# Two later layers of a three-layer block: values by token, scaled rotary tables, and half a convolution on ACT and POOL

## The chip, the cores and the metric

One core of one Trainium2 chip. The metric is the device time of one launch in microseconds. The median of three runs of the kernel before is 2020.88 us (2020.03 to 2021.06). Engines: PE is TensorE, DVE VectorE, ACT ScalarE, POOL GpSimd, SP SyncE.

## The reference, cut to what matters

A first block (a pooling mixer, a sparse attention of three branches, a gated feed-forward layer) works on 512 tokens of width 1024; two later layers follow. The change touches only the first part of each later layer: the input projection and the mixing that hangs on it.

```python
def mixing_layer(h, cos, sin, w_in, ...):
    u = jnp.einsum("bsd,de->bse", h, w_in)                # h = rmsnorm(x, mix_norm_g)
    a_b, a_c, a_x, q, k, v, c_in = jnp.split(u, offs, axis=-1)
    y_a = a_b * causal_depthwise_conv(a_c * a_x, short_conv_w)          # 3 taps, 256 wide
    q = apply_rope(q.reshape(b, s, 2, 4, 64), cos, sin)
    k = apply_rope(k.reshape(b, s, 2, 4, 64), cos, sin)
    o = diff_attention(q, k, v.reshape(b, s, 4, 128), lam)  # softmax(m=0) - lam * softmax(m=1)
    y_b = rmsnorm(o, diff_subln_g) * (1.0 - lam_init)
    c = c_in + glu_b
    c = c[..., :256] * jax.nn.sigmoid(c[..., 256:])
    c = causal_depthwise_conv(c, conf_dw_w) + conf_dw_b     # 31 taps, 256 wide
    y_c = jax.nn.silu(layernorm(c, conf_ln_g, conf_ln_b))
    return jnp.einsum("bse,ed->bsd", jnp.concatenate([y_a, y_b, y_c], -1), w_out)
```

## The kernel before

**Layout and arithmetic.** Everything is held feature by feature: 128 features on the partitions, the 512 tokens along a row. A weight chunk is eight blocks of 128x128 floats; it is split into a high part (`wh`, made by ACT with one copy, `head`) and the rest (`wl`, made by POOL in `rest` as two halves of 512 columns, `raw - wh`, L421). The input is split as well (`xh`, `xl`). A tile of 128 output features is three products over eight blocks: `wh` with `xh` (L450), `wh` with `xl` (L451), `wl` with `xh` (L470), 24 matmuls of 512 columns, into one PSUM bank. PE needs POOL's part only for the last eight. `wh` and `wl` hold two chunks each: ACT may write chunk n+2 when chunk n is done, and POOL subtracts chunk n+2 after that. Four semaphores carry this: `raw_landed`, `hi_ready`, `lo_ready`, `chunk_done`.

**Order of a later layer.** The order on each engine is written out by hand; there is no planner. The input projection takes 22 chunks. The first four are a group (`group`, L507, L508, L514): they fill four banks together, so that the feature blocks of the input are consumed as they come, and give `ca` and `cg`, the two halves of the gated unit (`glu`, L1731). Chunks 4 to 15 give, for each of four heads, a q tile, a k tile and a v tile; chunks 16 to 21 give the short convolution's tiles `a_c`, `a_x`, `a_b`, twice. Tiles go alternately to banks `G[0]` and `G[1]`; PE may start tile n when DVE has read tile n-2 (`tile_out`). After it come the output projection (eight chunks, the first four as a group in the order of rows `Y_ORDER`), the feed-forward layer's 44 chunks and its down projection.

**What is done beside the projection.** PE opens two slots in each chunk, one after the first eight matmuls and one after the first four low ones (`slot`, `layer_slots`). A head has steps 0 to 10, one in each half-chunk: steps 0 to 3 compute scores of one block of 128 queries (L839, L841), DVE takes the maxima (`peak`, L1739), ACT the exps (L1176), DVE combines the two softmaxes one step later (`combine`, L1746, L1748, L1252), PE transposes the result two steps later (L851), ACT copies it (`put`). Step 6 multiplies with the values (L858), steps 7 to 10 norm the head and split it into `yh`, `yl`. A score's step also waits until the exps of the step before have read its banks. Heads start every six half-chunks, at slot 14.

**Rotation.** DVE takes a q or k tile out of its bank times the norm's scale `rstd` into `ybuf` (`take`, L1295; with 0.125 for q, L1255) and multiplies it with `cos2` into `tmp3` (L1811). PE rotates `ybuf` with a matrix (`rotate_l`, L828), and DVE multiplies with `sin2` and adds (`rot_end`, L1708, L1710). A v tile is taken in the same way, transposed by PE (`turn_v`, L816) and copied by ACT into `lv`.

**The 31-tap convolution** runs on DVE alone for both groups of 128 channels (`taps`, L1722 and L1252, 2 x 31 instructions of 128x512 a layer), between the steps by a written plan (`TAP_PLAN`). Before dependent operations DVE has an explicit drain (L1718 and others).

## Time and profile before

| | |
|---|---|
| median of three runs | 2020.88 us |
| the profiled execution's own time | 2020.96 us |
| its span, first to last instruction | 2019.2 us |
| mean granted TensorE clock | 0.981 |
| busy: PE, DVE, ACT, POOL | 1930.6 (96%), 990.2 (49%), 690.8 (34%), 880.9 us (44%) |
| layer 1: first matmul of the group, end of chunk 3, first matmul of the output projection | 764.08, 787.2, 970.92 us |
| layer 2: the same stage | 1381.56 to 1591.06 us |

How to read it. A row of a window gives its length, then for each engine busy time and, in brackets, the number of instructions, then the granted clock (1.00 is full), the share of the DMA engines and GB/s. A row of waits says who waited, for whom, the total in us, how often, and the longest. A row of instructions by line gives the tile written and the tiles read, the shape, the count, then busy us and the mean ns of one, and the idle time of the engine just before them with what ended it. A row of a source view gives minimum, median and maximum ns. A row of the timeline gives start and length in us, and in square brackets the idle time before it. PEld is the weight load, POOLq the sequencer of POOL. A line such as L1252 is a helper's (`fma`) and serves several callers; the tile tells them apart.

### The profile page before, as it was taken

What the parts mean: (1) busy time and instruction counts of PE and PEld (TensorE: products, weight loads), DVE (VectorE), ACT (ScalarE), POOL (GpSimd) and SP (SyncE); (2) the same over time, 40 slices, a digit from 0 to 9 for tenths busy, and PEclk for the clock granted to TensorE, in tenths of its full rate; (3) what the DMA queues carried; (4) which work ended last, traced back from release to release, by engine and by line L of the source; (5) the groups of instructions that cost most, each with busy time, mean ns of one, the idle gap of its engine ahead of it and who ended that gap; (6) DMA issues with size and microseconds to landing.
All of it is one profiled execution on the core that took longest, in us unless ns stands there. A gap on an engine that the chain in (4) does not pass through costs nothing.

```text
span 2019.2 us, 28668 instructions
## 1 busy us (share of the span) xinstructions
PE 1930.6 (96%) x8702; PEld 1521.7 (75%) x8702; DVE 990.2 (49%) x1398; ACT 690.8 (34%) x1084; POOL 880.9 (44%) x630
## 2 busy tenths in 40 slices
PE   6999999999999998988999999999897999999996
PEld 5866678878888887656888888887565888888885
DVE  7667654466664214886443333123878343333213
ACT  4245553333232222344433333223243343232222
POOL 4222224446555554322445455454222344554554
PEclk9999999999999999999999999999899999999998
DMA  6111112222222332111222322332111222222232
GB/s 238 63 53 43 43 63 94 94 84 93 95 103 94 104 104 84 53 47 52 80 94 93 102 95 93 104 104 95 52 45 51 73 90 98 93 93 97 101 104 83
DMA packets 48952, 173.89 MB, mean 86 GB/s; under 512 B 5488, under 2 KB 6512, under 8 KB 48624
## 3 DMA queue, kind: packets, MB, share of 16 engines
q1 hardware_dynamic: 48880, 172.96, 25.6%
q8 instruction: 42, 0.69, 0.1%
q14 instruction: 30, 0.25, 0.0%
HBM read 169.82 MB, written 2.10 MB: 85 GB/s over the span
## 4 chain that ended last, share of the span: by engine, by line
PE 85%; DVE 7%; DVEq 4%; issue 2%; ACT 2%; DMA 0%; ACTq 0%; SPq 0%
PE bank L450 21%; PE bank L470 21%; PE bank L451 21%; PE bank L507 3%; PE bank L514 3%; PE bank L508 3%; DVEq L1718 1%; PE bank L484 1%; PE bank L684 1%; PE bank L490 1%; PE bank L485 1%; DVEq L1810 1%; PE bank L713 1%; PE bank L531 1%; PE bank L727 1%
## 5 line engine op out<-in xcount | busy, mean ns | idle before, releaser
L421 POOL TENSOR_TENSOR wl<-raw,wh x626 | 880.7, 1428 | 1124.6 <-ACT wh L919 1124.4
L919 ACT ACTIVATE wh<-raw 128x1024 fp32r (+1 forms) x313 | 331.8, 1060 | 872.0 <-PE bank L470 740.5
L450 PE MATMUL bank<-xh,wh 128*128 128x512 f32 x1400 | 565.6, 404 | 5.6 <-DVE tmp L1295 5.6
L451 PE MATMUL bank<-xl,wh 128*128 128x512 f32 x1400 | 554.1, 396 | 0.0
L470 PE MATMUL bank<-xh,wl 128*128 128x512 f32 x1400 | 359.9, 396 | 0.0
L450 PEld LDWEIGHTS bank<-xh,wh 128*128 128x128 f32 x1400 | 268.7, 192 | 67.5 <-issue 7.0
L451 PEld LDWEIGHTS bank<-xl,wh 128*128 128x128 f32 x1400 | 268.9, 192 | 60.6 <-issue 4.9
L470 PEld LDWEIGHTS bank<-xh,wl 128*128 128x128 f32 x1400 | 262.6, 190 | 56.3 <-issue 3.0
L450 PE MATMUL bank<-hh,wh 128*128 128x512 f32 x528 | 208.0, 394 | 0.0
L451 PE MATMUL bank<-hl,wh 128*128 128x512 f32 x528 | 208.0, 394 | 0.0
L1295 DVE TENSOR_TENSOR ybuf<-bank,rstd 128x512 f32<-128x512 f32 x111 | 76.2, 687 | 231.3 <-PE bank L470 229.3
L1664 DVE TENSOR_TENSOR tmp<-tmp,ybuf 128x512 f32<-128x512 f32 x66 | 109.8, 1664 | 74.3 <-ACT tmp L1136 74.1
L1626 DVE TENSOR_TENSOR xs<-xs,bank 128x512 f32<-128x512 f32 (+1 forms) x48 | 32.1, 684 | 226.4 <-PE bank L470 178.0
L470 PE MATMUL bank<-hh,wl 128*128 128x512 f32 x528 | 134.8, 394 | 0.0
L451 PEld LDWEIGHTS bank<-hl,wh 128*128 128x128 f32 x528 | 98.7, 187 | 24.5
L450 PEld LDWEIGHTS bank<-hh,wh 128*128 128x128 f32 x528 | 98.7, 187 | 24.4
L470 PEld LDWEIGHTS bank<-hh,wl 128*128 128x128 f32 x528 | 98.7, 187 | 24.4
L1252 DVE SCALAR_TENSOR_TENSOR conv<-cpad,par,conv 128x512 f32<-128x512 f32 x120 | 102.0, 891 | 6.7 <-issue 2.1
L507 PE MATMUL bank<-xh,wh 128*128 128x512 f32 x192 | 76.7, 400 | 9.4 <-ACT wh L919 8.5
L919 ACT ACTIVATE hh<-tmp 128x512 f32 (+1 forms) x66 | 41.7, 632 | 120.3 <-DVE tmp L1664 120.3
L1666 DVE TENSOR_TENSOR hl<-tmp,hh 128x512 f32 (+1 forms) x66 | 51.1, 774 | 59.8 <-ACT hh L919 59.8
L508 PE MATMUL bank<-xl,wh 128*128 128x512 f32 x192 | 75.8, 395 | 0.0
(273 smaller groups left out, 2099.4 us busy)
## 6 DMA issues: line engine op xcount, KB each, us to landing
raw<-in_weights SPq DMA_DIRECT2D x313, 512.0 KB, 3.3
xs<-in_x SPq DMA_DIRECT2D x4, 512.0 KB, 6.9
out_t<-xs SPq DMA_DIRECT2D x8, 256.0 KB, 2.2
w1k<-in_w SPq DMA_DIRECT2D x1, 1024.0 KB, 9.5
w1v<-in_w SPq DMA_DIRECT2D x1, 1024.0 KB, 10.5
shifted<-kvraw SPq DMA_DIRECT2D x8, 124.0 KB, 2.4
posi<-in_positions SPq DMA_DIRECT2D x2, 256.0 KB, 8.6
cst<-in_consts SPq DMA_DIRECT2D x1, 290.0 KB, 5.2
```

What stands on the lines that cost most here:

```text
L421: x_ = pool.tensor_tensor(wl[:, :, :].rearrange("p s n -> p (s n)")[:, two], raw[:, cols((v % 4) * (CB * P) + h * half, half)], wh[:, :, : ...
L450: mm(b[:, :], w, kh(k), start=first and k == 0, stop=False)
L451: mm(b[:, :], w, kl(k), start=False, stop=False)
L470: i = mm(b[:, :], wl[:, s, (blk0 + k) * P:(blk0 + k + 1) * P], kh(k), start=False, stop=last and k == blocks - 1)
L507: mm(X4[a][:, :], w, kh(k), start=k == 0, stop=False)
L508: mm(X4[a][:, :], w, kl(k), start=False, stop=False)
L514: i = mm(X4[a][:, :], wl[:, s, (4 * kk + a) * P:(4 * kk + a + 1) * P], kh(2 * c + kk), start=False, stop=c == 3 and kk == 1)
L919: return act.activation(o, i, ACT.Copy, scale=scale)
L1252: return stt(out=o, in0=a, scalar=s, in1=b, op0=ALU.mult, op1=ALU.add)
L1295: return tt(o, b[:, :], rstd[:, :], ALU.mult).then_inc(tile_out, 1)
L1664: tt(tmp[:, 1, :], tmp[:, 0, :], ybuf[:, 0, :], ALU.mult).then_inc(R["prod_ready"], 1)
L1666: tt(flat(hl)[:, cols(j * S, S)], tmp[:, 1, :], flat(hh)[:, cols(j * S, S)].bitcast(F32), ALU.subtract).then_inc(R["h_lo"], 1)
```

## The change

Only the later layers change.

1. **Values token by token.** Chunks 4 to 7 are one group, `vgroup`: the input's token block is the stationary operand and 512 weight columns move, so four banks receive tokens on the partitions and all four heads' values along a row. ACT copies them into `lv`, each token with its own scale (`s_recip`). `turn_v` and DVE's takes of v are gone. The weights are laid out anew for it.
2. **Rotary tables hold the norm's scale.** DVE multiplies `cos2` and `sin2` once a layer with the broadcast scale into `cosr`, `sinr`. ACT copies a raw q or k tile from its bank to `ybuf`; DVE multiplies the bank with `cosr` into `tmp3`, and that frees the bank.
3. **Half the convolution off VectorE.** Channels 0 to 127 stay on DVE (one instruction a tap, with most taps before the first rotary tile). For channels 128 to 255 ACT makes each tap's product into `tprod` (two buffers) and POOL adds it, between its subtractions, from chunk 5 on: three taps a chunk up to chunk 9, then two.
4. **A head every four half-chunks**, starting at slot 21 of 43 (two slots a chunk, counted from the first chunk). Older heads go first in a slot, and PE's transposes stand ahead of the scores. The values' products go to bank `ROT` in place of `OUT`. The norm's statistics are numbered anew, and `Y_ORDER` is changed so that head 3 is the fifth row.

```diff
-HEAD0 = 7
-Y_ORDER = ("head0", "head1", "head2", "ya0", "head3", "ya1", "conv0", "conv1")
+HEAD_SLOT = 21
+Y_ORDER = ("head0", "head1", "ya0", "head2", "head3", "ya1", "conv0", "conv1")
@@ layer_slots
-        s = 2 * (n - HEAD0) + half
-        yield s, [(h, s - 6 * h) for h in (3, 2, 1, 0) if 0 <= s - 6 * h <= 10]
+        s = 2 * n + half
+        yield s, [(h, s - HEAD_SLOT - 4 * h) for h in range(4) if 0 <= s - HEAD_SLOT - 4 * h <= 10]
@@ gpsimd
+                def tap(k):
+                    if k == 0:
+                        pool.tensor_scalar(conv[:, 1, :], cpad[:, 1, 0:S], c2("dw_w", TAPS), c2("dw_b", 1),
+                                           ALU.mult, ALU.add)
+                    else:
+                        pool.drain()
+                        pool.wait_ge(R["tap_prod"], Count(k).loop(l, TAPS - 1).value())
+                        pool.tensor_tensor(conv[:, 1, :], conv[:, 1, :], tprod[:, k % 2, :], ALU.add)\
+                            .then_inc(R["tap_added"], 1)
+                done = 0
+                for n in range(T_LIN):
+                    if n == 5:
+                        pool.wait_ge(R["glu_out"], Count(1).loop(l, 1).value())
+                    rest(T + n)
+                    if n >= 5:
+                        upto = min(done + (3 if n < 10 else 2), TAPS)
+                        for k in range(done, upto):
+                            tap(k)
+                        done = upto
@@ tensor
+            def vgroup(t, n, hooks):
+                for c in range(4):
+                    s = (t + c).even()
+                    pe.wait_ge(hi_ready, (t + (c + 1)).value())
+                    for i in range(NT):
+                        if c == 0 and i >= 2:
+                            pe.wait_ge(tile_out, (n + (i - 1)).value())
+                        for kk in range(2):
+                            k = 2 * c + kk
+                            w = wh[:, s, kk * S:(kk + 1) * S]
+                            mm(VB[i][:, :], xh[:, k, i * P:(i + 1) * P], w, start=k == 0, stop=False)
+                            mm(VB[i][:, :], xl[:, k, i * P:(i + 1) * P], w, start=False, stop=False)
+                    pe.wait_ge(lo_ready, (t + (c + 1)).value())
+                    for i in range(NT):
+                        for kk in range(2):
+                            k = 2 * c + kk
+                            x_ = mm(VB[i][:, :], xh[:, k, i * P:(i + 1) * P], wl[:, s, kk * S:(kk + 1) * S],
+                                    start=False, stop=k == KD - 1)
+                    x_.then_inc(chunk_done, 1)
...
@@ scalar
+                def products(n):
+                    for k in range(made[0], min(made[0] + n, TAPS)):
+                        if k == 1:
+                            act.wait_ge(R["glu_out"], L1.value())
+                        if k > 2:
+                            act.wait_ge(R["tap_added"], Count(k - 2).loop(l, TAPS - 1).value())
+                        copy(tprod[:, k % 2, :], cpad[:, 1, k:k + S], scale=c2("dw_w", TAPS + k))\
+                            .then_inc(R["tap_prod"], 1)
+                    made[0] += n
...
+                        if n >= 5:
+                            products(2 if n < 10 and half == 0 else 1)
...
+                    if 8 <= n < 16:
+                        i, m = n - 8, n - 4
+                        if i >= 2:
+                            act.wait_ge(rot_ready, Count(6 + i).loop(l, 8).value())
+                        b = QK0[i] if i < 2 else G[(N + m).even()]
+                        copy(ybuf[:, i % 2, :], b[:, :]).then_inc(R["rope_in"], 1)
                     head(T + (n + 2))
+                    if n == 7:
+                        act.wait_ge(recip_ready, (U0 + 1).value())
+                        for i in range(NT):
+                            copy(lv[:, :, i, :], VB[i][:, :].rearrange("p (h d) -> p h d", d=P),
+                                 scale=s_recip[:, i:i + 1]).then_inc(R["v_out"], 1)
@@ vector
-                TAP_PLAN = {4: (2, 1), 5: (1, 1), 6: (2, 1), 19: (2, 2)}
+                TAP_PLAN = {4: (0, 2), 5: (2, 2), 6: (2, 2), 7: (2, 2), 8: (2, 2), 9: (2, 2)}
...
+                tt(cosr, BC[:, :], cos2[:, :], ALU.mult)
+                tt(sinr, BC[:, :], sin2[:, :], ALU.mult).then_inc(bc_read, 1)
...
-                        take(tl, nl_, ybuf[:, n % 2, :], scale=0.125 if what == 0 else None)
-                        if what < 2:
-                            dve.drain()
-                            tt(tmp3[:, 0:S], ybuf[:, n % 2, :], cos2[:, :], ALU.mult)
+                        dve.wait_ge(R["rope_in"], Count(i + 1).loop(l, 8).value())
+                        if i % 2:
+                            tt(tmp3[:, 0:S], b[:, :], cosr, ALU.mult).then_inc(tile_out, 1)
+                        else:
+                            mul3(tmp3[:, 0:S], b[:, :], 0.125, cosr).then_inc(tile_out, 1)
```

## Rows read from the trace of the kernel before

**Rows 1.** The page, part 4: shares of the chain that ended last.

```profile
PE 85%; DVE 7%; DVEq 4%; issue 2%; ACT 2%; DMA 0%; ACTq 0%; SPq 0%
```

**Rows 2.** Windows: layer 1's stage, its part after chunk 10, layer 2's stage.

```profile
764.08:970.92 206.84, 182.42 (x832) 135.12 (x830) 146.60 (x229) 73.95 (x142) 63.92 (x45) 0.95 0.17 59
854.95:970.92 115.97, 101.34 (x476) 73.89 (x474) 84.73 (x134) 45.40 (x90) 31.43 (x22) 0.96 0.15 51
1381.56:1591.06 209.50, 185.08 (x831) 137.16 (x832) 146.47 (x229) 73.62 (x142) 63.40 (x44) 0.93 0.18 59
```

**Rows 3.** Windows: one bare chunk, and one head period of three chunks.

```profile
787.20:792.66 5.46, 5.46 (x25) 4.50 (x24) 4.04 (x6) 3.68 (x4) 2.54 (x2) 1.00 0.26 98
844.27:876.13 31.86, 28.23 (x135) 19.64 (x135) 26.39 (x44) 13.93 (x30) 9.23 (x6) 1.00 0.17 57
```

**Rows 4.** Waits of PE over the whole span.

```profile
PE bank L828 <- DVE ybuf L1295: 14.8, 6, 2.8
PE bank L828 <- DVE ybuf L1255: 10.5, 2, 5.2
PE bank L851 <- DVE lp L1252: 9.7, 2, 4.9
...
PE bank L839 <- ACT lp L1176: 6.4, 8, 1.0
PE bank L816 <- DVE ybuf L1295: 6.0, 4, 2.0
```

**Rows 5.** PE by line in the same period: the value transposes.

```profile
L816 PE MATMUL bank<-cst,ybuf 128*128 128x128 f32 x4 | 0.6, 272 | 0.0
```

**Rows 6.** DVE by line in the head period of rows 3.

```profile
L1252 DVE SCALAR_TENSOR_TENSOR conv<-cpad,par,conv 128x512 f32<-128x512 f32 x12 | 9.5, 832 | 0.7 <-issue 0.2
L1739 DVE TENSOR_REDUCE small<-bank 128x1 f32<-128x128 f32 (+3 forms) x8 | 3.5, 481 | 1.5 <-PE bank L841 1.5
L1748 DVE TENSOR_SCALAR lp<-lp,small 128x128 f32<-128x128 f32 (+3 forms) x4 | 3.3, 814 | 0.3
L1811 DVE TENSOR_TENSOR tmp<-ybuf,cos 128x512 f32<-128x512 f32 x2 | 2.6, 1315 | 0.2
L1252 DVE SCALAR_TENSOR_TENSOR lp<-lp,small 128x128 f32<-128x128 f32 (+3 forms) x4 | 2.2, 552 | 0.3
L1708 DVE TENSOR_TENSOR tmp<-bank,sin 128x512 f32<-128x512 f32 x2 | 1.4, 684 | 0.0
L1295 DVE TENSOR_TENSOR ybuf<-bank,rstd 128x512 f32<-128x512 f32 x2 | 1.4, 680 | 0.0
...
L1272 DVE RECIPROCAL small<-small 128x4 f32<-128x4 f32 x1 | 0.2, 178 | 2.3 <-ACT small L936 2.3
```

**Rows 7.** ACT by line in layer 1's stage: a 128x512 copy.

```profile
L919 ACT ACTIVATE yh<-lo__109 128x512 fp32r<-128x512 f32 x4 | 2.5, 627 | 0.9 <-DVEq L1769 0.9
```

**Rows 8.** Source views of L421 and L1252, whole span: ns min/median/max.

```profile
L421 POOLq FUSED_REGOPS  x939: 57/74/161, 8.5 to 2002.7; - x188
...
L421 POOL TENSOR_TENSOR wl<-raw,wh x626: 1262/1292/1933, 8.9 to 2004.0; - x157
...
L1252 DVE SCALAR_TENSOR_TENSOR conv<-cpad,par,conv x120: 739/750/1853, 794.4 to 1561.6; 128x512 f32<-128x512 f32 x120
```

**Rows 9.** Timeline of DVE and POOL in layer 1, 791 to 798 us.

```profile
791.11 2.12 DVE L1731 SCALAR_TENSOR_TENSOR cpad<-ca,par,cg 128x512 f32<-128x512 f32 x2 [1.20 <-ACT cg L1210]
...
794.57 1.69 POOL L421 TENSOR_TENSOR wl<-raw,wh  x1 [2.56 <-ACT wh L919]
...
795.06 1.75 DVE L1252 SCALAR_TENSOR_TENSOR conv<-cpad,par,conv 128x512 f32<-128x512 f32 x1
...
796.89 1.59 DVE L1252 SCALAR_TENSOR_TENSOR conv<-cpad,par,conv 128x512 f32<-128x512 f32 x1
```

**Rows 10.** Timeline of PE in layer 1: a late stall, and a layer norm's sums.

```profile
941.14 0.44 PE L851 MATMUL bank<-cst,lp 128*128 128x128 f32 x1 [4.87 <-DVE lp L1252]
...
954.96 1.84 PE L531 MATMUL bank<-cst,conv 128*128 128x1 f32 x16
```

More of the change, by code:

```diff
@@ L425, in rest @@
                 x_.then_inc(lo_ready, 1)
-            with pool.Fori(0, T_ALL + 2) as t:
+            with pool.Fori(0, T_BLOCK1) as t:
                 rest(Count(0).loop(t, 1))
+            with pool.Fori(0, LAYERS) as l:
+                T = Count(T_BLOCK1).loop(l, T_LAYER)
+                def tap(k):
[17 more added lines that the diff above has]
+                        done = upto
+                with pool.Fori(T_LIN, T_LAYER) as t:
+                    rest(T.loop(t, 1))
+            for t in range(T_ALL, T_ALL + 2):
+                rest(Count(t))
         @block.tensor
@@ L803, in lam_sum @@
                     pe.wait_ge(R["lam_in"], L1.value())
[L804 removed]
+                    pe.wait_ge(tile_out, (N + 3).value())
+                    mm(TR[:, 0:2], ones, lamp, start=True, stop=True).then_inc(R["lam_psum"], 1)
                 RO = Count(7).loop(l, 8)
@@ L893, in slot @@
-                    if s == 26:
-                        pe.wait_ge(R["conv_done"], L1.value())
-                        ln_stats(U0 + 5, conv)
-                    if s == 27:
-                        spread(U0 + 5, lambda i: s_recip[:, i:i + 1].to_broadcast([P, P]))
-                    if s == 28:
+                    if half == 0 and 9 <= n < 17:
+                        rotate_l(n - 9)
+                    if s == 38:
+                        pe.wait_ge(R["conv_done"], L1.value())
+                        pe.wait_ge(R["tap_added"], Count(TAPS - 1).loop(l, TAPS - 1).value())
+                        ln_stats(U0 + NORM_LN[0], conv)
@@ L904, in _ @@
                 xgroup(T, feed, {(1, 1): lambda: x_stats(U0, feed), (2, 0): lambda: x_spread(U0)})
-                for n in range(4, T_LIN):
-                    xk(T + n, N + n, slots=[lambda: slot(n, 0), lambda: slot(n, 1)], lag=5 if n < 6 else 1)
-                tb, nb = out_and_ffn(T + T_LIN, N + T_LIN, (yh, yl), (R["y_lo"], Count(0).loop(l, KD)), U0 + 7,
+                vgroup(T + 4, N, {(1, 0): lam_sum})
+                for m in range(4, N_LIN):
+                    n = m + 4
+                    if m == 4:
+                        pe.wait_ge(R["lam_exp"], L1.value())
+                    if m == 6:
+                        pe.wait_ge(R["v_out"], Count(NT).loop(l, NT).value())
+                    xk(T + n, N + m, slots=[lambda: slot(n, 0), lambda: slot(n, 1)],
+                       lag={4: 0, 5: 1, 6: 2, 7: 3}.get(m, 1), bank_=QK0[m - 4] if m < 6 else None)
@@ L1212, in _ @@
                 for n in range(4, T_LIN):
-                    for s, steps in layer_slots(n):
-                        if n == 6 and s % 2 == 0:
+                    for half, (s, steps) in enumerate(layer_slots(n)):
+                        if s == 11:
                             act.wait_ge(R["lam_psum"], L1.value())
-                            act.activation(lame, POOLB[:, 0:2], ACT.Exp).then_inc(R["lam_exp"], 1)
+                            act.activation(lame, TR[:, 0:2], ACT.Exp).then_inc(R["lam_exp"], 1)
+                        if s == 38:
+                            act.wait_ge(R["ya_ready"], Count(1).loop(l, 2).value())
+                            y_head("ya0", ya[:, 0, :])
@@ L1699, in _ @@
                 ts(sub_gain, c2("sub_g"), c2("lam_init", 1), None, ALU.mult)
-                x_norm(U0)
+                recips(U0, NT)
+                dve.wait_ge(bc_ready, (U0 + 1).value())
+                dve.tensor_copy(rstd[:, :], BC[:, :])
+                dve.memset(sqacc[:, :], 0.0)
+                dve.drain()
                 SS = Count(4 * NU).loop(l, 32)
```

169 lines of the change are left out of this document (85 added, 84 removed).

## The prediction

> **What bounds the kernel now.** First the page: the chain that ended last is 85% TensorE (PE) [rows 1], so time is lost where PE waits. The change touches only the input projection of the two later layers, so next come the windows of those stages: layer 1 from the first matmul of its group to the first of the output projection, 206.84 us, and layer 2, 209.5 us [rows 2]. In them PE is busy 182.4 and 185.1 us, at a mean granted clock of 0.95 and 0.93 of full. A bare chunk of 24 matmuls takes 5.46 us [rows 3]; 22 of them are 120 us, the rest is attention and losses. The waits of PE name the cause: the rotation L828 waits for `ybuf` from VectorE (DVE) 14.8 + 10.5 us, the transposes L851 of the probabilities 9.7, the scores L839 for exps 6.4, the value transposes L816 6.0 [rows 4]. These lines exist only in these two stages: 47.4 of the 48.8 us that PE is idle there. DVE is not full, but works in order: in one head period of three chunks (844.27 to 876.13) it is busy 26.39 of 31.86 us, PE 28.23, ScalarE (ACT) 13.93, GpSimd (POOL) 9.23 [rows 3].
>
> **The change, part by part.**
>
> *Values token by token.* The four value tiles become one group with the same 96 matmuls of 512 columns: no change for PE. What goes is `turn_v`, 0.6 us a head [rows 5], and its wait, 3.0 us a layer. DVE loses four takes of 0.68 [rows 6]. ACT still makes four copies of a bank, now scaled. Two of the group's banks are free, two come free with the first two takes, 0.7 and 1.4 us after its start, and are needed after 1.8 and 2.7. Hidden under the first two banks' matmuls; were DVE late, the price is one take.
>
> *Rotary tables with the scale in them, raw copy on ACT.* Two DVE products more a layer, 1.4 us after the GLU, when nothing waits for DVE. Per rotated tile DVE does one product from the bank in place of a take and a product; ACT adds a copy, eight a layer, 0.63 each by its nearest row [rows 7]. The rotation no longer waits for DVE but for ACT, which stands behind two exps and a tap product there. Of the 12.6 us a layer of L828 some 9 go; I leave 0.8 a head.
>
> *Channel 1 of the convolution on ACT and POOL.* DVE loses 31 taps of 0.75 [rows 8]. ACT gains 30 products of 0.63. POOL gains 31 operations of 128x512, the shape of its own halves: 1.29, from 1.26 to 1.93 [rows 8]. Before nearly each stand a drain, register work and a wait, which the halves don't have: at least the 0.07 of one FUSED_REGOPS, at most what the slowest half takes over the usual, 0.64; I take 0.3, half way. A tap is 1.3 to 2.6 then, and I take 1.6 alone.
>
> The rows show that this is free for neither engine. While POOL subtracts, DVE's taps take 1.75 and 1.59 in place of 0.75, and POOL's half 1.69 in place of 1.29 [rows 8, 9]: side by side, one of each goes through in about 1.7. The Trainium skill (SBUF — State Buffer, "SBUF: two separate sides") calls the pair of ports that both use an exclusive lock for a whole instruction, where the loser "fully blocks". By that a pair would cost 0.75 + 1.29 = 2.04; the trace's 1.7 is softer, in the same direction.
>
> DVE's channel 0 is pulled ahead: 18 taps stand before the first rotary tile with nothing to hold them, so from 794 DVE runs them back to back at 1.75, until 825.5. POOL's part of chunks 5 to 9 is two halves and three taps: beside DVE's taps 3.4 + 3 x 2.0 = 9.3 us (rounded down), afterwards 2.6 + 3 x 1.6 = 7.4. PE's bare chunk is 5.46, so POOL bounds chunks 6 to 10. On layer 1's clock: the GLU ended at 793.2 beside POOL [rows 9], and ends at 792.7 without; only then may POOL subtract chunk 5, done 795.9, needed 796.3: hidden. Its taps last until 801.1. Low parts are ready for chunk 6 at 804.5, 7 at 813.8, 8 at 823.1; then, DVE being done, 5.4 + 2.9 and 4.8 + 2.9 (one meeting each left): 9 at 831.3, 10 at 839.0. The eight low matmuls (a third of 5.46) and one score (0.6, an estimate from the four transposes of [rows 5]) later chunk 10 ends, 841.4. Before it ended at 854.95: a gain of 13.5. PE alone would be there at about 828.
>
> *A head every four half-chunks, from slot 21.* Eleven chunks remain. PE's work: the old period has 28.23 busy for three chunks and one head; less `turn_v` 0.6 and a chunk 5.5 that is 22.1 for two chunks and a head, so 11.1 of attention a head. Sum: 11 x 5.5 = 60.5; four heads 44.4, less the slot of it already done, 2.8; the layer norm's two sums of 1.84 [rows 10] and two spreads of 0.5, 4.7: 106.8.
>
> DVE in the new period: 26.39, less all conv taps 9.5, less three takes 2.0 and two cos products 2.6, plus two taps 1.5 and two products 1.4: 15.2 [rows 3, 6]. In the old period POOL's six operations cost DVE, on L1811, 2.6 for 1.4, and on the conv taps, 9.5 for 9.0; on L1748 about 1.2 of its 3.3: 2.9 in all, 0.5 each. POOL now has eight in a shorter period: 4 in place of L1748's 1.2 makes 18. ACT: 13.93 plus four products and two copies of 0.63, at most 17.7. PE binds with 22.1, but three in-order engines hand over in every slot. What is late next: the first score of a head stands one slot (5.5 us of PE) behind its own key's rotation. In that slot DVE first waits 2.3 for the root of the head two before, then has its reciprocal 0.2, a combine 1.4, a peak 1.0, a tap 0.8, the rotation's end 1.4 [rows 6], and one meeting with POOL 0.5: 7.6, so 2.1 late for two of four heads, 1.05 a period. With 0.8 for the rotation and 0.5 for exps that is 2.4 a period: 24.5, and over 3.5 periods 8.4. The stall behind the short convolution's block (4.87 at 941.14 [rows 10]) moves; I leave 3 for it. After chunk 10: 106.8 + 8.4 + 3 = 118.2; before 115.97 [rows 2]. This part gives back 2.2: the old losses were small here.
>
> *Order of heads and rows.* Head 3 ends in the last half-chunk; the output projection takes it as its fifth row, 10.9 us on, `conv0` at 16.4. Hidden under its first two chunks; without them one DVE subtraction, 0.7. SP's queue keeps number and size of its loads. POOL's program is longer, for which no row has a price: 0, bounded by 3 us (a start of a chunk missed in each layer).
>
> **Sum.** Layer 1: 841.4 + 118.2 = 959.6 against 970.92, gain 11.3. Layer 2 has the same program: twice, 22.6. The profiled execution takes 2020.96 for its span of 2019.2, and the median is 2020.88, so nothing is carried over. 2020.9 - 22.6 = 1998.3; I say 1999.
>
> Unknowns: POOL's tap at 1.3 in place of 1.6 is 4 us a layer (-8), at 2.6 its ends come up to 12 later (+24). A period without losses is -8.4 a layer (-17); its ceiling is a rival.
>
> **Rivals.**
>
> *PE-bound (0.26).* Waits spread DVE and POOL so that they meet little, and the hand-overs hide. For it: PE's 22.1 over DVE's 18. Against it: DVE's unheld taps. POOL alone still needs 7.4 a loop, so chunk 10 ends at 835; then 106.8: 941.8, gain 29.1 a layer: 1963.
>
> *DVE bound under POOL (0.17), the other side.* In a period DVE has 13 operations that read SBUF for both inputs, or one input at double rate (combine 8, rotation's ends 2, taps 2, a remainder 1). If all meet POOL at 0.95 each, as 0.75 became 1.7 [rows 9]: 15.2 - 1.2 + 12.4 = 26.4, and with the idle 2.3 for the root 28.7. Four heads cost 4.2 more each, 16.8 a layer: 976.4, 5.5 later than before: 2032. It decides from a period of 27.3 on. Against it: POOL idles about half of a period.
>
> *The lock as that page has it (0.09).* Each of DVE's 18 taps costs POOL 0.35 more, 6.3 a layer, and about 5 again in the attention part: 11.3 a layer, 2021, no change. It is the skill's sentence that asks for it (same page and section); the rows of 1.7 speak against.
>
> **How the numbers follow.** Forecast (about 1985 to 2014) 0.48. Within 0.2% (4 us) a measurement can't tell from no change. Faster: 0.48 + 0.26 = 0.74. Same: 0.07, of the lock. Slower: 0.17 + 0.02 = 0.19. The range takes in the PE-bound case and stops short of 2032: 1961 to 2026.
>
> **What would show it.** In chunks 6 to 10 of each later layer PE waits for `wl` before the low matmuls, 2 to 4 us each, POOL is at 90%, DVE's taps take 1.6 to 1.75, and chunk 10 ends 54 us after chunk 3. L816 is gone. Where the rotation waits, it is for ACT. Head periods are 24 to 25 us, the first score of heads 2 and 3 waits for `lk`. The stages take 196 and 198 us. It is wrong if chunks 6 to 10 take 5.5 us each (POOL's tap is cheaper or hidden), or if a period is above 27 with DVE full.

## The result, and the profile after

The changed kernel takes 1987.1 us (median of 4 runs, 1985.0 to 1989.4) against 2021.0: the ratio is 0.9828, 95% interval 0.9814 to 0.9843, and the medians are 33.9 us apart. The prediction said 1999 (1961 to 2026). The profiled execution takes 1989.08 for its span of 1987.3.

The page of the changed kernel, its first and fourth parts (beside [rows 1]): VectorE (DVE) is busy 25.8 us less, ScalarE (ACT) 44.5 and GpSimd (POOL) 89.5 us more; in the chain, the share of DVE's sequencer is halved and POOL's sequencer is new.

```profile
PE 1918.2 (97%) x8670; PEld 1515.1 (76%) x8670; DVE 964.4 (49%) x1316; ACT 735.3 (37%) x1160; POOL 970.4 (49%) x692
...
PE 81%; DVE 6%; POOLq 3%; issue 3%; DVEq 2%; ACT 2%; POOL 1%; DMA 1%; ACTq 0%; SPq 0%
```

Windows of the changed kernel, in the columns of [rows 2]: layer 1's stage from the group's first matmul to the first of the output projection; its part from the GLU's end to the end of chunk 10; the part after chunk 10; one head period (first score of head 1 to that of head 2); and layer 2's stage.

```profile
763.89:957.02 193.13, 179.15 (x816) 134.56 (x815) 136.31 (x188) 96.27 (x180) 108.73 (x76) 0.96 0.19 63
792.60:839.30 46.70, 40.02 (x158) 29.94 (x157) 42.79 (x35) 22.41 (x35) 42.66 (x29) 0.93 0.20 68
839.30:957.02 117.72, 110.42 (x528) 80.69 (x527) 84.21 (x135) 63.37 (x135) 55.42 (x39) 0.96 0.17 54
857.90:881.68 23.78, 21.94 (x109) 15.21 (x107) 17.26 (x30) 15.05 (x33) 11.70 (x9) 1.00 0.14 45
1367.53:1559.40 191.87, 175.91 (x815) 131.20 (x815) 135.62 (x188) 95.83 (x180) 108.72 (x75) 0.98 0.19 64
```

The stages are shorter by 206.84 - 193.13 = 13.7 and 209.50 - 191.87 = 17.6 us. Together that is 31.3 of the 31.9 us between the two profiled executions, so the rest of the program accounts for 0.6. Of layer 1's 13.7, PE idles 10.4 less (24.4 before, 14.0 now) and is busy 3.3 less; of layer 2's 17.6 it is 8.5 and 9.2. Busy time fell because 16 transposes a layer are gone and because the granted clock is higher (0.95 to 0.96, 0.93 to 0.98).

Waits of PE in the changed kernel, in the form of [rows 4] (rows of other stages left out). L816 is gone; L881 is the rotation, L892 the first instruction of a head's scores, L582 and L506 the low matmuls, which read POOL's halves `wl`; L599 is the spread of a norm.

```profile
PE bank L892 <- DVE lk L1793: 10.2, 6, 2.4
...
PE bank L582 <- POOL wl L428: 8.3, 4, 2.8
...
PE bank L599 <- DVE small L1348: 4.2, 4, 1.9
PE bank L506 <- POOL wl L428: 3.4, 5, 0.8
PE bank L881 <- ACT ybuf L972: 3.1, 6, 0.8
PE bank L892 <- ACT lp L1229: 2.1, 2, 1.0
```

The first scores of the four heads (L894) stand at 837.73, 857.90, 881.68 and 907.29. Below, the stage is split at them: 73.8 us from the start to the first (the *front*), periods of 20.2, 23.8 and 25.6, and 49.7 from the last to the output projection.

The timeline of POOL in layer 1 (start, length, then idle time before): two halves of a chunk and three taps take 7.28, 8.65, 8.39, 7.58 and 8.47 us from one chunk's halves to the next (in the first of them one tap is the initial product L443, in all others the three are additions, L448). Where additions follow each other beside DVE's taps they start 1.68 to 1.71 apart: 1.45 to 1.48 of work and 0.22 to 0.23 in which POOL waits for nothing that the profile shows.

```profile
799.90 3.41 POOL L428 TENSOR_TENSOR wl<-raw,wh 128x512 fp32r<-128x512 f32 x2
803.89 1.29 POOL L448 TENSOR_TENSOR conv<-conv,tprod 128x512 f32<-128x512 f32 x1 [0.57 <-issue]
805.41 1.48 POOL L448 TENSOR_TENSOR conv<-conv,tprod 128x512 f32<-128x512 f32 x1 [0.23 <-issue]
807.10 1.48 POOL L448 TENSOR_TENSOR conv<-conv,tprod 128x512 f32<-128x512 f32 x1 [0.22 <-issue]
808.55 3.37 POOL L428 TENSOR_TENSOR wl<-raw,wh 128x512 fp32r<-128x512 f32 x2
...
816.94 2.53 POOL L428 TENSOR_TENSOR wl<-raw,wh 128x512 fp32r<-128x512 f32 x2
```

DVE beside it, 13 taps of channels 0 to 127 back to back, 1.66 us each:

```profile
794.28 21.56 DVE L1328 SCALAR_TENSOR_TENSOR conv<-cpad,par,conv 128x512 f32<-128x512 f32 x13
```

And PE: two waits for the low parts, and what came after the second.

```profile
803.37 2.14 PE L582 MATMUL bank<-wl,xh 128*128 128x512 f32 x8 [1.42 <-POOL wl L428]
...
811.98 3.78 PE L582 MATMUL bank<-wl,xh 128*128 128x512 f32 x8 [2.83 <-POOL wl L428]
815.56 0.63 PE L486 MATMUL bank<-xh,wh 128*128 128x512 f32 x1
815.99 0.63 PE L487 MATMUL bank<-xl,wh 128*128 128x512 f32 x1
```

After the 2.83 us wait the same eight matmuls take 3.78 instead of 2.14 us, and the next start 0.43 apart instead of 0.23: the granted clock is on its lower level (1.2 of 2.4 GHz). A window of these 8 us shows it: 23 matmuls, clock 0.62, where 8 busy us before held 37.

```profile
788.00:796.00 8.00, 8.00 (x37) 6.63 (x36) 6.54 (x10) 6.56 (x8) 3.31 (x3) 1.00 0.08 32
...
812.00:820.00 8.00, 8.00 (x23) 6.32 (x24) 7.70 (x6) 5.39 (x8) 7.18 (x6) 0.62 0.19 66
```

So in the 8 us behind the wait PE does 14 matmuls fewer, some 3 us of work, and the profile counts them as busy time. The kernel did not lose these 3 us. The version *reciprocals last* (below) is the same up to the first score. It waited 2.88 us at the same place and went on at full pace; its PE then waited 1.83 us for the next low part. Its front is as long, at a clock of 1.00 instead of 0.95. First the changed kernel's front, then the waits and the front of that version.

```profile
763.89:837.73 73.84, 67.16 (x282) 52.61 (x280) 51.61 (x51) 32.18 (x42) 51.97 (x37) 0.95 0.22 73
```

```profile
814.38 2.11 PE L582 MATMUL bank<-wl,xh 128*128 128x512 f32 x8 [2.88 <-POOL wl L428]
...
821.95 2.11 PE L506 MATMUL bank<-xh,wl 128*128 128x512 f32 x8 [1.83 <-POOL wl L428]
...
766.29:840.14 73.85, 64.61 (x282) 50.46 (x280) 51.61 (x51) 32.05 (x42) 51.97 (x37) 1.00 0.22 72
```

POOL sets the pace there, and the clock only decides whether PE's slack shows as busy or as idle. Why the level fell behind one wait and not behind the other is open: it fell behind one of 2.87 us at this place in the run with the raw copy on VectorE, and did not behind one of 2.68 in the run with VectorE's taps spread.

### The profile page after: what moved, and what is told of

Read it like the earlier page. It is cut to its first block, busy times and chain, and to the rows that moved or that the text cites. A ratio compares the mean times of both kernels' runs of the same rounds, so it can differ in the third digit from the quotient of the medians.

```text
span 1987.3 us, 28229 instructions
## 1 busy us (share of the span) xinstructions
PE 1918.2 (97%) x8670; PEld 1515.1 (76%) x8670; DVE 964.4 (49%) x1316; ACT 735.3 (37%) x1160; POOL 970.4 (49%) x692
## 3 DMA queue, kind: packets, MB, share of 16 engines
q1 hardware_dynamic: 48880, 172.96, 25.8%
## 4 chain that ended last, share of the span: by engine, by line
PE 81%; DVE 6%; POOLq 3%; issue 3%; DVEq 2%; ACT 2%; POOL 1%; DMA 1%; ACTq 0%; SPq 0%
PE bank L506 21%; PE bank L486 20%; PE bank L487 20%; PE bank L543 3%; PE bank L550 3%; PE bank L544 3%; POOLq L446 3%; PE bank L520 1%; PE bank L744 1%; PE bank L526 1%; PE bank L521 1%; DVE lp L1832 1%; PE bank L773 1%; POOL wl L428 1%; PE bank L787 1%
## 5 line engine op out<-in xcount | busy, mean ns | idle before, releaser
L428 POOL TENSOR_TENSOR wl<-raw,wh (+1 forms) x626 | 883.6, 1433 | 921.7 <-ACT wh L972 907.9
L486 PE MATMUL bank<-xh,wh 128*128 128x512 f32 x1336 | 533.2, 399 | 5.5 <-DVE tmp L1371 5.5
L487 PE MATMUL bank<-xl,wh 128*128 128x512 f32 x1336 | 524.3, 392 | 0.0
L506 PE MATMUL bank<-xh,wl 128*128 128x512 f32 x1336 | 343.2, 396 | 3.4 <-POOL wl L428 3.4
L486 PEld LDWEIGHTS bank<-xh,wh 128*128 128x128 f32 x1336 | 253.7, 190 | 65.5 <-issue 7.9
L506 PEld LDWEIGHTS bank<-xh,wl 128*128 128x128 f32 x1336 | 249.6, 189 | 63.8 <-issue 7.1
L487 PEld LDWEIGHTS bank<-xl,wh 128*128 128x128 f32 x1336 | 253.5, 190 | 56.4 <-issue 3.8
L1371 DVE TENSOR_TENSOR ybuf<-bank,rstd 128x512 f32<-128x512 f32 x95 | 65.3, 688 | 227.2 <-PE bank L506 225.2
L506 PE MATMUL bank<-hh,wl 128*128 128x512 f32 x528 | 134.8, 394 | 0.0
L448 POOL TENSOR_TENSOR conv<-conv,tprod 128x512 f32<-128x512 f32 x60 | 85.4, 1424 | 80.7 <-ACT tprod L972 72.6
L506 PEld LDWEIGHTS bank<-hh,wl 128*128 128x128 f32 x528 | 98.7, 187 | 24.5
L486 PEld LDWEIGHTS bank<-hh,wh 128*128 128x128 f32 x528 | 98.7, 187 | 24.4
L487 PEld LDWEIGHTS bank<-hl,wh 128*128 128x128 f32 x528 | 98.7, 187 | 24.4
L543 PE MATMUL bank<-xh,wh 128*128 128x512 f32 x192 | 76.8, 400 | 9.1 <-ACT wh L972 8.4
L1328 DVE SCALAR_TENSOR_TENSOR conv<-cpad,par,conv 128x512 f32<-128x512 f32 x60 | 80.4, 1340 | 4.9
```

The costliest lines, as they stand in the source:

```text
L428: x_ = pool.tensor_tensor(wl[:, :, :].rearrange("p s n -> p (s n)")[:, two], raw[:, cols((v % 4) * (CB * P) + h * half, half)], wh[:, :, : ...
L448: pool.tensor_tensor(conv[:, 1, :], conv[:, 1, :], tprod[:, k % 2, :], ALU.add)\
L486: mm(b[:, :], w, kh(k), start=first and k == 0, stop=False)
L487: mm(b[:, :], w, kl(k), start=False, stop=False)
L506: i = mm(b[:, :], wl[:, s, (blk0 + k) * P:(blk0 + k + 1) * P], kh(k), start=False, stop=last and k == blocks - 1)
L543: mm(X4[a][:, :], w, kh(k), start=k == 0, stop=False)
```

## The experiments

Each kernel ran beside runs of the kernel before on the same chip (2022.3 to 2023.0 us there, against the 2021.0 beside which the changed kernel ran). A difference between medians of different groups carries that shift of 1 to 2 us; the ratios don't. All change one thing in the changed kernel unless said otherwise; diffs are cut to the core.

### What each half of the convolution costs, and where

**Channels 128 to 255 left out (taps 1 to 30), in both kernels.** In the changed kernel ACT's and POOL's part goes, in the kernel before VectorE's.

```diff
# changed kernel
-                        upto = min(done + (3 if n < 10 else 2), TAPS)
+                        upto = 1
-                            products(2 if n < 10 and half == 0 else 1)
# kernel before
-                            else:
+                            elif c == 0:
                                 x_ = fma(conv[:, c, :], ...
```

> The changed kernel with taps 1 to 30 of channels 128 to 255 left out: no products on ACT, no additions on POOL, the rest as it is (output not the reference's). Theory: POOL's taps alone bound chunks 6 to 10 (chunk 10 ends at 839.3 on layer 1's clock, PE alone would be there at 828), and meet DVE later on. Then chunk 10 ends at 828 to 829, the rest of the stage gets some 2 to 3 us shorter, 14 us a layer: 1987 - 28 = 1959. Rival 1, DVE's 18 unheld taps bound those chunks: they stay above 6.5 us each, 1975 to 1985. Rival 2, the convolution's place doesn't matter, the gain is the head spacing: 1983 or more.

> The kernel before with taps 1 to 30 of channels 128 to 255 left out on DVE, all else as before (output not the reference's). Theory: what PE lost before (24 us idle a layer) was DVE being late with takes and combines, and half of the taps is 23 us of DVE a layer, so PE's idle time falls from 24 to 6 to 10 us a layer, and less of it runs at the lower clock: 18 us a layer, about 1985, as good as the whole change. Rival, the old order of heads sets the pace: L828's and L851's waits remain, 2010 or more.

Measured: 1954.8 us (ratio 0.9666, 0.965 to 0.9682) and 1987.7 (0.9827, 0.9811 to 0.9843). Both near their forecasts (1959 and 1985). By the ratios the second channel block costs 35 us in the old structure, on VectorE, and 33 in the new one, on ScalarE and GpSimd. The intervals allow 3 to 4 us either way, so putting it on two other engines is not shown to have made it cheaper. Without that block in the changed kernel PE waits for no low part, chunk 10 ends near 830 and the front is 64.1 us instead of 73.8. That is within 2 us of the 828 of the prediction's "PE alone": the term "POOL bounds chunks 6 to 10" is right.

**Both halves on VectorE, in the new structure.** Nothing of the convolution on ACT and POOL; DVE's plan (taps per half-chunk) as changed, each tap twice.

```diff
-                            x_ = fma(conv[:, 0, :], cpad[:, 0, k:k + S], w, conv[:, 0, :])
+                        for c in range(2):
+                            w = c2("dw_w", c * TAPS + k)
+                                x_ = fma(conv[:, c, :], cpad[:, c, k:k + S], w, conv[:, c, :])
```

> The changed kernel with part 3 undone: both halves of the convolution on DVE by the changed kernel's own plan of taps, none on ACT and POOL. Theory (POOL was the bound of the front, DVE has slack of 5 to 6 us in a head period of 24): DVE needs 36 taps of 0.75 before the rotary tiles, done at about 825 in place of 823; chunk 10 ends at 831 to 833 in place of 839.3, head periods stay at 24: 7 us a layer faster, about 1973. Rival, DVE needs the relief, as in the kernel before: the first rotations and the periods wait for DVE, 27 us and more a period, 2000 to 2015.

Measured: 1995.9 (0.9865, 0.9849 to 0.9882). The theory of 1973 missed by 23, by one wait a layer. DVE runs 36 operations unheld before the first rotation's end and four more before the second, for which PE waits. The theory priced them at 0.75 and had the 36 done at 825; beside POOL's halves 26 of them take 1.07 each, and the 36 are done at 834.6. The rival had the first rotations wait for VectorE, but its periods of 27 did not occur.

```profile
799.36 27.92 DVE L1323 SCALAR_TENSOR_TENSOR conv<-cpad,par,conv 128x512 f32<-128x512 f32 x26
...
PE bank L879 <- DVE tmp L1326: 27.9, 2, 13.9
```

The periods behind it are 19.3, 23.1 and 24.2 us, a little shorter than with POOL's help (20.2, 23.8, 25.6). So VectorE has room for all 62 taps; it is their place in front of the first rotation that hurts.

**The same with VectorE's taps spread.** 13 taps before chunk 10 and two a chunk after it, with the two orders of the last version below (reciprocals and sums).

```diff
-                TAP_PLAN = {4: (0, 2), 5: (2, 2), 6: (2, 2), 7: (2, 2), 8: (2, 2), 9: (2, 2)}
+                TAP_PLAN = {4: (0, 2), 5: (1, 1), 6: (1, 1), 7: (1, 1), 8: (1, 1), 9: (2, 1)}
-                        taps(TAP_PLAN.get(n, (1, 0))[half])
+                        taps(TAP_PLAN.get(n, (1, 1))[half])
```

> The changed kernel with both halves of the convolution on VectorE, nothing of it on ScalarE and GpSimd, and VectorE's taps spread (13 before chunk 10, 2 a chunk after), reciprocals and sums ordered as in best1. Theory (splitting the convolution over engines was not what gave the gain; VectorE has room for 2 x 31 taps at 1.3 us once they stand where it is free): 1970 to 1980, the 13.9 us wait a layer of the version with both halves on VectorE and the old plan gone. Rival (VectorE is then the bound of the attention part: 2 taps of both halves a chunk, 5.2 us, on top of its 17 a head): periods of 27 or more between first scores, 1995 to 2005.

Measured: 1979.6 (0.9791, 0.9777 to 0.9804). No convolution on POOL or ACT at all, and faster than the changed kernel: the intervals don't meet. The two orders have a part in that, since the reciprocals' order alone takes the changed kernel to nearly the same ratio (0.9794, below); the fair comparison is with the last version, which has the same orders and the split. The rival (DVE-bound periods of 27) fell: they are 20.4, 22.7, 22.7. The row of the taps shows why the split relieves VectorE so little. First this kernel, then the changed one; by source line: count, ns minimum/median/maximum.

```profile
L1323 DVE SCALAR_TENSOR_TENSOR conv<-cpad,par,conv x120: 741/751/1847, 797.6 to 1523.6; 128x512 f32<-128x512 f32 x120
```

```profile
L1328 DVE SCALAR_TENSOR_TENSOR conv<-cpad,par,conv x60: 750/1605/1790, 794.3 to 1532.4; 128x512 f32<-128x512 f32 x60
```

By the groups by line, 120 taps cost DVE 103.1 us here (900 ns on average), and 60 cost 80.4 (1340 ns) in the changed kernel. Moving half the taps away took 23 us from DVE, not 52, because those left run beside POOL's additions.

**Channels 0 to 127 for 8 columns only**, so that POOL's additions run with DVE mostly free.

```diff
-                            x_ = fma(conv[:, 0, :], cpad[:, 0, k:k + S], w, conv[:, 0, :])
+                            x_ = (fma(conv[:, 0, 0:8], cpad[:, 0, k:k + 8], w, conv[:, 0, 0:8]) if k < TAPS - 1 else
+                                  fma(conv[:, 0, :], cpad[:, 0, k:k + S], w, conv[:, 0, :]))
```

> The changed kernel with VectorE's taps 1 to 29 of channels 0 to 127 computed for 8 columns only, so that GpSimd's additions run with VectorE mostly free. If the two engines hold each other up at their memory: GpSimd's addition falls from 1.45 to 1.3 us and below, its loop of a chunk with three taps from 8.5 to 8, and no wait of TensorE for GpSimd's low parts is over 1.5 us; first score 68 to 70 us after the group's first matmul (73.8 before), time 1968 to 1976. If GpSimd's pace is its own: additions stay at 1.45, TensorE waits for the low parts as before (3 to 4 us twice), first score 72 to 74, and only the wait for the keys of heads 2 and 3 (10.2 us in all) goes: 1975 to 1980.

Measured: 1967.1 (0.9724, 0.9709 to 0.9739), the first theory, a little below its range. POOL's timeline: additions of 1.29, 1.52 apart, halves 1.26 each, a loop of 7.0 to 7.4 instead of 7.6 to 8.65. The longest wait for a low part is 1.63 us (not over 1.5 was expected) and the front 67.9. Without POOL's additions it was 64.1, so POOL's own pace holds the front too, by about 4 us, even when VectorE leaves it alone.

```profile
809.38 2.52 POOL L428 TENSOR_TENSOR wl<-raw,wh 128x512 fp32r<-128x512 f32 x2
812.12 1.29 POOL L448 TENSOR_TENSOR conv<-conv,tprod 128x512 f32<-128x512 f32 x1 [0.23 <-issue]
813.64 1.29 POOL L448 TENSOR_TENSOR conv<-conv,tprod 128x512 f32<-128x512 f32 x1 [0.23 <-issue]
815.16 1.29 POOL L448 TENSOR_TENSOR conv<-conv,tprod 128x512 f32<-128x512 f32 x1 [0.22 <-issue]
816.42 2.50 POOL L428 TENSOR_TENSOR wl<-raw,wh 128x512 fp32r<-128x512 f32 x2
```

So each engine slows the other: DVE's tap goes from 0.75 to 1.66 us, POOL's addition from 1.29 to between 1.45 and 1.48, its half from 1.26 to 1.7.

**Both cut**: channels 128 to 255 without taps 1 to 30, and channels 0 to 127 with 8 columns.

> The changed kernel with taps 1 to 30 of channels 128 to 255 left out and taps 1 to 29 of channels 0 to 127 computed for 8 columns only: nearly no convolution on any engine. It is the floor of what any placing of the taps can reach. If TensorE's own work is that floor: 1945 to 1954, barely under the version without channels 128 to 255 (1954.8), periods between first scores 21 to 22.5 us. If VectorE's taps of channels 0 to 127 were a second bound behind GpSimd's: 1935 to 1944.

Measured: 1947.5 (0.963, 0.9615 to 0.9645), the first theory. Layer 1's stage is 170.9 us, 169.5 of them PE's, at full clock; periods are 17.6, 21.8, 21.8. This is what placing taps can reach at most: 39.6 us below the changed kernel. The prediction's 22.1 of PE's work in a period was right within 0.5.

```profile
765.56:936.44 170.88, 169.49 (x816) 129.69 (x814) 100.74 (x188) 77.84 (x150) 58.97 (x46) 1.00 0.22 72
```

### Where the raw copy belongs

**VectorE copies the raw q or k tile to `ybuf`** in place of ScalarE.

```diff
-                        copy(ybuf[:, i % 2, :], b[:, :]).then_inc(R["rope_in"], 1)
+                        dve.tensor_copy(ybuf[:, i % 2, :], b[:, :]).then_inc(R["rope_in"], 1)
```

> The changed kernel with part 2 half undone: DVE, not ACT, makes the raw copy of each q and k tile into ybuf, before its product with the table. Theory: the copy costs DVE 0.7 more a tile, and the rotation again waits for DVE's place in its order, 1 to 1.5 us a tile: 8 to 12 us a layer, about 2007. Rival, DVE idles 1.8 us a tile waiting for ACT's copy anyway, so its own copy fits there: 1983 to 1991, no change.

Measured: 1988.5 (0.9834, 0.9816 to 0.9852), no change: the rival's time, and the theory of 2007 missed. The wait changes its name and size (rotation for DVE 8.7 us in all, against 3.1 for ACT), and the waits for the keys give part of it back (7.2 against 10.2). In layer 1 the front is 3.2 us longer and the three periods together 3.3 shorter (19.0, 23.0, 24.2). Which engine makes that copy is not what gained.

### Two bounds in the front

Three edits, alone and together. *Later additions*: ACT and POOL do two taps a chunk in chunks 5 to 9 and three from 10 on. *Spread*: VectorE's plan as in the diff above. *Reciprocals last*: VectorE's reciprocal of a norm's root, for which it waits in order, comes after the other heads' steps of its slot and its tap.

```diff
# later additions
-                        upto = min(done + (3 if n < 10 else 2), TAPS)
+                        upto = min(done + (2 if n < 10 else 3), TAPS)
-                            products(2 if n < 10 and half == 0 else 1)
+                            products(2 if n >= 10 and half == 0 else 1)
# reciprocals last
-                    if step == 7:
-                        recips(U0 + NORM_OF_HEAD[h], NT)
...
                         taps(TAP_PLAN.get(n, (1, 0))[half])
+                        for h, step in steps:
+                            if step == 7:
+                                recips(U0 + NORM_OF_HEAD[h], NT)
```

> The changed kernel with another plan for channels 128 to 255: two taps a chunk in chunks 5 to 9, three from chunk 10 on (before: three, then two), for ACT's products and POOL's additions alike. Theory: POOL's part of a front chunk falls from 8.5 (measured: halves 3.4, taps 1.69 apart) to 6.8, so chunk 10 ends at about 831.5 on layer 1's clock in place of 839.3; behind it POOL has 9.7 of work in chunks of 12 and meets DVE more, which gives 2 to 3 us back: 5 us a layer, 1977. Rival, the third tap lands on the critical hand-overs of ACT and DVE in the attention part and costs as much there as the front gains: 1985 to 1990.

> The changed kernel with DVE's taps of channels 0 to 127 spread: 13 before chunk 10 and two a chunk from there on, in place of 22 and one. Theory: DVE is done with its unheld taps 8 us earlier, so POOL's halves take 2.6 in place of 3.4 in two or three of the front chunks, 1.5 to 2 us; from chunk 10 on the second tap falls mostly into DVE's 1.8 us of waiting for ACT's copy: 1983 to 1986. Rival, DVE's order is tight there (each tap stands ahead of the product that frees the bank): 1992 and more.

> The changed kernel; on DVE the reciprocal of a head's root (step 7) stands behind the other heads' steps and the tap of its half-chunk, not ahead of them. Theory: the first scores of heads 2 and 3 wait 1.6 and 2.3 us for lk because DVE stood idle for that root; both waits go, head periods 23.8 and 25.5 become 22.5 and 23.5: 3 to 4 us a layer, 1980. Rival, lk is late for DVE's other work or for ACT (exps, table loads), the wait moves to the exps or to the spread: 1986 to 1990.

> All three together: later taps on POOL and ACT, reciprocals last, DVE's taps spread. If the three causes are apart from each other the gains add: chunk 10 ends at 830, periods of 23: 1970 to 1974. If the attention part gets too dense (two DVE taps, three POOL taps a chunk), periods go to 25 and it stays at 1980.

| version | us | ratio (interval) | front | periods | last part |
|---|---|---|---|---|---|
| changed kernel | 1987.1 | 0.9828 (0.9814 to 0.9843) | 73.8 | 20.2, 23.8, 25.6 | 49.7 |
| later additions | 1992.5 | 0.9848 (0.9831 to 0.9864) | 72.4 | 19.7, 24.5, 26.6 | 49.9 |
| spread | 1992.3 | 0.985 (0.9834 to 0.9867) | 71.7 | 20.6, 23.8, 25.6 | 51.9 |
| reciprocals last | 1981.2 | 0.9794 (0.9778 to 0.981) | 73.9 | 20.2, 22.0, 22.8 | 48.6 |
| all three | 1974.6 | 0.9768 (0.9752 to 0.9784) | 64.6 | 21.5, 23.2, 24.8 | 51.0 |

The first two theories missed: both edits were expected to shorten front and time (1977, and 1983 to 1986). The fronts fell by only 1.4 and 2.1 us, and the time did not fall; it is rather longer, though both intervals overlap that of the changed kernel. The rivals describe what came instead: with later additions the second and third periods are 0.7 and 1.0 longer; with the taps spread the last part is 2.2 longer, of it 1.1 in which the layer norm's sums wait for a tap. The third theory and the fourth held (1981.2 for 1980, and 1974.6, just above 1970 to 1974). With later additions the longest waits for low parts in layer 1 fall to 1.2 and 1.1 us, but the rotation and the scores then wait for VectorE's taps:

```profile
829.56 2.07 PE L881 MATMUL bank<-ybuf,cst 128*128 128x512 f32 x2 [2.32 <-DVE tmp L1331]
837.37 0.29 PE L892 MATMUL bank<-msk 128*128 128x128 bf16 x2 [2.42 <-DVE lk L1793]
```

With VectorE's taps spread, VectorE stands idle for 12 us before the first rotation's end (the ACT copy it names waits for PE, and PE for POOL), so there POOL alone holds the front:

```profile
824.66 0.69 DVE L1331 SCALAR_TENSOR_TENSOR tmp<-bank,tmp 128x512 f32<-128x512 f32 x1 [12.46 <-ACT ybuf L972]
```

Each bound alone gives a front of about 72; only with both gone does it fall, to 64.6. (The reciprocals' order leaves the front as it is, 73.9, so the fall is not its doing.) That order is a matter of its own, worth 6 to 7 us: in the changed kernel VectorE waits 1.83 us for the root in a slot in which the scores of the next head wait for VectorE.

```profile
876.43 0.18 DVE L1348 RECIPROCAL small<-small 128x4 f32<-128x4 f32 x1 [1.83 <-ACT small L989]
...
880.64 0.69 DVE L1793 TENSOR_TENSOR lk<-tmp,tmp 128x512 f32<-128x512 f32 x1
```

```profile
881.47 0.28 PE L892 MATMUL bank<-msk 128*128 128x128 bf16 x2 [1.59 <-DVE lk L1793]
```

### The best version

All three edits, with the additions two a chunk up to chunk 15 and three after, the reciprocals after the head steps but ahead of the tap, and a norm's spread last among PE's steps of a slot.

```diff
+                        upto = min(done + (2 if n < 16 else 3), TAPS)
+                            products(2 if n >= 16 and half == 0 else 1)
-                    for h, step in steps:
+                    for h, step in sorted(steps, key=lambda hs: hs[1] == 8):
                         head_step(h, step)
```

> The comb version (1974.6) with three orders changed: GpSimd adds two taps a chunk until the sixteenth and three from there, VectorE takes the reciprocal of a root after the head steps but ahead of its convolution taps, and TensorE's sums (spread) come last in their half-chunk. Theory (what is left of the wait is small orders, each worth 1 to 3 us a layer: in comb TensorE waited 9.7 us in all for the reciprocals' small tile in front of the spread, and VectorE's taps stand ahead of them): 1966 to 1971, spread wait under 4 us in all. Rival (the wait only moves to the next instruction, because the head period is near TensorE's own 22 us already): 1973 to 1977.

Measured: 1969.5 (0.9744, 0.9731 to 0.9757): 17.6 us below the changed kernel, 52.8 below the kernel before beside it (2022.3). Its interval overlaps that of "all three" (0.9752 to 0.9784) by a little, so the last 5 us are not quite clear of noise. The spread's wait, expected under 4 us, is still 5.7 (it was 9.7; 2.4 of either lie outside the two stages), so the theory's total held and this part of it did not. Windows of it, the whole stage of layer 1 and a period:

```profile
764.34:945.37 181.03, 171.89 (x816) 128.92 (x814) 131.02 (x188) 95.88 (x180) 108.16 (x76) 1.00 0.21 67
...
871.40:894.68 23.28, 21.87 (x109) 15.21 (x107) 20.38 (x34) 15.69 (x35) 11.86 (x8) 1.00 0.15 46
```

Against the changed kernel's stage PE idles 4.8 us less (14.0 to 9.1) and is busy 7.3 us less for the same 816 matmuls, at a clock of 1.00 instead of 0.96. That is not a gain of 7.3 by the clock: of the 12.1 us the front gives 9.3 and the three periods 3.8 (20.6, 21.9, 23.3), and the last part (50.7) takes 1.0 back. In the changed kernel itself layer 1 and layer 2 differ by 3.2 us of PE's busy time at clocks of 0.96 and 0.98, and by only 1.3 us of length, 1.1 of it in the last part; front and first two periods agree within 0.02. The front is 64.5 us, the floor 62.6; with the same orders the split beats both halves on VectorE by 10 us (1969.5 to 1979.6). In layer 1 the periods of the two are equal in sum (65.8), the front is 1.8 and the last part 6.0 us shorter with the split.

## Why the prediction was right

**The sum.** Chunk 10 was to end at 841.4 in layer 1 and ended at 839.3; after it 118.2 us were expected and 117.7 measured. "Gain 11.3, twice" was 13.7 and 17.6, so the forecast is 12 us too long. Of these, 2.4 in each layer are the size of the terms above, nearly all of it at chunk 10. Another 3.9 are "the same program: twice", said of two stages whose rows already differed: the kernel before lost 2.7 us more in layer 2, at a clock of 0.93 [rows 2], and the changed one is 1.3 us shorter there than in layer 1, at 0.98. The rest is 2.0 by which the profiled execution lies above its kernel's median, 0.7 of rounding, and 0.6 outside the two stages.

**POOL bounds chunks 6 to 10: right, with its parts off.** POOL's tap beside DVE was put at 2.0 and is 1.69, alone 1.6 and is 1.52; its loop beside DVE's taps was put at 9.3 and is 7.6 to 8.65, alone at 7.4 and is 7.0 to 7.4 (the run with 8 columns). Low parts were ready at 803.3, 811.9, 819.5, 827.9 and 836.4, against 804.5, 813.8, 823.1, 831.3 and 839.0. Two errors of opposite sign are in that. Up to chunk 8 the sum is 3.6 us late: it adds 0.3 for drain, register work and wait to the 1.7 in which a pair goes through, while the measured 1.68 to 1.71 hold POOL's 0.22 already. The last two loops it made 8.3 and 7.7, "DVE being done"; VectorE ran five more taps between the rotations, until 835.3, and they are 8.5 each. Together 2.6 us are left: the mechanism held, and that the error is so small is partly luck. PE's waits are smaller than "2 to 4 us each": 1.42, 2.83, none, 0.80 and 0.79. Of the 11.3 us by which chunk 10 ended behind the 828 of a bare PE, 6.7 are idle time, and some 3 more are PE at the lower clock, which took the place of waiting (above) and not of work.

**DVE's unheld taps: right in size, wrong in weight.** They take 1.66 us, as forecast (1.6 to 1.75), and VectorE is done with them at 825.1. But the sum treated them only as what slows POOL. The experiments show them as a second bound of the front within a microsecond or two of POOL's. They are one only at that price: with POOL's additions gone the same 13 taps take 17.1 us (1.32 each, beside POOL's halves) in place of 21.6, and the front is 64.1.

**The lock.** By the Trainium skill (SBUF — State Buffer, "SBUF: two separate sides") the loser of the shared ports "fully blocks"; by an estimate from that rule a tap and an addition together would take at least 0.75 + 1.29 = 2.04 us. Measured, one of each goes through in 1.66 to 1.71, so the rule overstates the price here. The time of 2021 that the rival gave is refuted. The Trainium skill (Perfetto Trace Analysis, "Optimizing Scalar/DVE Operations") also warns that moving work between these two engines "might not help". Here it helped a little: the split was worth 7.5 us by the ratios with the plan as changed (8.8 by the medians, 1995.9 to 1987.1) and 10.1 with the plan spread, of the 41 us that this half costs on VectorE (1995.9 against 1954.8 without it).

**The head period.** Forecast 24.5, of it PE 22.1; measured 20.2, 23.8, 25.6 (mean 23.2), PE 21.9. DVE is busy 17.3 of 23.8 (forecast 18), ACT 15.1 (at most 17.7). The named cause is right: the first scores wait for `lk` 10.2 us in all, 1.15, 1.59 and 2.29 in layer 1 (forecast 2.1 for heads 2 and 3), and for heads 2 and 3 behind the wait for the root. It was tested: with the reciprocals last these waits fall to 2.3, all of it head 1's, which has no root ahead of it; the spread of the norm waits longer for that (8.1 in all against 4.2). The rotation waits for ACT, 3.1 in all where 0.8 a head was left (6.4). The stall behind the short convolution, left at 3, is gone: no wait of PE after chunk 10 is above 2.5 in either layer. PE's work was forecast well: 106.8, and 105.8 in the version with reciprocals last, at a clock of 1.00. In the changed kernel PE is busy 110.4 us of these 117.7, at 0.96, and idle 7.3, not 11.4. So fewer waits than forecast and more matmuls at the lower level gave nearly the forecast sum, and that agreement is partly luck. Layer 2, at 0.99, takes 116.5.

**What gained.** For the most part not half of the convolution on other engines. With both halves on VectorE the new structure already takes 1995.9, 27 us less than the kernel before beside it (2023.0), and 1979.6 with taps and orders placed well. Of PE's 10.4 us less idle time in layer 1, 7.3 lie behind chunk 10 (14.6 to 7.3) and 3.1 before it. The part behind chunk 10 is 1.8 us longer all the same, because it now holds 528 matmuls and not 476: a part of the attention has moved there. Of the rest of the change the raw copy's engine gave nothing. Values token by token, the table product and the closer heads were not run apart, so their shares stay open.

**The rivals.** PE-bound (1963) did not occur here; it is nearly what the best version reaches (1969.5), and 1947.5 with almost no taps is the floor. DVE bound under POOL (2032) did not occur: periods stay below 27.3, also with three additions a chunk on POOL (26.6 at most) and with all 62 taps on VectorE (24.2).

## What to carry to other kernels

Work moved between two engines that slow each other has to be priced on both: the taps left on VectorE went from 0.75 to 1.66 us where POOL's additions ran beside them, so moving half of them took only a fifth off the time it spends on taps. Where two chains end within a microsecond or two of each other, an edit to one shows nothing or a loss; test the pair. Busy time of PE is not comparable between executions without the clock beside it: the same front held 67.2 us of it at a clock of 0.95 and 64.6 at 1.00, in the same 73.8 us. So read a gain from the length of each part, not from busy time; and order an engine so that an instruction that must wait for another stands behind those that someone waits for.

## What was not expected of the hardware

- An addition of 128x512 on POOL takes 1.29 us alone and 1.45 to 1.48 beside VectorE's taps, but successive ones start 1.52 and about 1.69 apart: 0.22 to 0.23 us pass in front of each, where the program has a drain and a wait, and once, before the third addition of layer 1, 0.57 (0.32 in layer 2).
- The slowing is uneven: VectorE's tap grows by 0.91 us, POOL's addition by 0.16 to 0.19, its halves by 0.44 each. The two engines then run in step, 1.66 against 1.69.
- The wait of 1.42 us that ended at 803.37 left PE's matmuls at full pace; after the wait of 2.83 that ended at 811.98 they ran on the lower level until about 818. The same place in two other versions: a wait of 2.88 and one of 2.68, and full pace behind both. The length of the wait alone does not decide it.
